# A two-block transformer forward pass: another order inside the attention steps, a second buffer for the copied transposes, late filling, and split bank waits

## The chip, the cores and the metric

The kernel runs on one core of a Trainium2 chip. The metric is the device time of one execution in microseconds (us). One launch computes the whole function. The five engines of the core have their own instruction queues and run in program order: TensorE (PE, with PEld for its weight loads), VectorE (DVE), ScalarE (ACT), GpSimd (POOL), and SyncE (SP), whose queue issues most of the transfers. They meet only through semaphores that count up.

## The reference, cut to what matters

Two transformer blocks of different kinds follow each other on a sequence of 512 tokens of width 1024, in float32. The parts that the change touches are the two attentions and what stands after them:

```
# block 1, 8 heads of 64 in 2 key/value groups; all 8 selection blocks are taken (min(16, 8)) and the
# window of 512 covers the whole sequence, so two of the three branches are plain causal attentions
s = einsum('bqgrd,bgqkld->bgrqkl', qc, ksel) * scale ; p = masked_softmax(s, m_sel)      # selected
s = einsum('bqgrd,bkgd->bgrqk', qc, kwc) * scale     ; p = masked_softmax(s, m_win)      # window
return gc[..., 0:1] * o_cmp + gc[..., 1:2] * o_sel + gc[..., 2:3] * o_win
x = x + (gate_pool * y_pool + gate_nsa * y_nsa) @ w_out
gate_pre, val = split(rms_norm(x) @ w_up) ; x = x + (silu(conv3(gate_pre)) * val) @ w_down

# block 2: a gated delta rule in 4 heads, and 8 heads of causal banded attention with a bias by distance
qkv = silu(conv4(concat(qa, ka, va)))
s = einsum('bqhd,bkhd->bhqk', qc, kc) * scale + bias ; p = softmax(s) ; o = einsum(..., p, vc)
mix = sigmoid(ga) * (oa @ w_branch_a) + sigmoid(gb) * (ob @ w_branch_b) ; x = x + mix @ w_out
u = conv3(rmsnorm(x) @ w_up) + b ; x = x + (silu(gate) * up) @ w_down ; return rmsnorm(x)
```

## The kernel before, in words

Activations lie transposed: features on the 128 partitions, the 512 tokens along the row. A weight matrix comes in chunks, each a column of 128x128 tiles for one output tile of 128 features. To keep float32 accuracy each product is made of three matmuls over a high and a low half (`product`, lines 1569 to 1580): high weights by high activations (L1576), high weights by low activations (L1577), low weights by high activations (L1578). A chunk of eight contraction tiles is 24 matmuls of 512 columns. For each chunk SP loads `w_raw` (`load`, L562), ACT makes `w_hi` (`high`, L739), and DVE or POOL makes `w_lo` (`low`, L540); each of these tiles has two slots, so a chunk's load, high and low wait for the chunk two before it. The order of all this is written out by hand, with one function per stage and engine.

The PSUM banks are ACC (0 and 1, chunk results), BS (2, 3), BT (4, 5) and BO (6, 7).

`attention` is written once per engine (PE L1669, ACT L835, DVE L1176) and used twice: att1 has 24 units (4 pairs of heads, 3 sets of query blocks, 2 branches), att2 has 12. A unit passes through a pipeline of steps; in step s

- PE makes the scores of unit s into BS (L1678), then the value products of unit s-3 from `at_pt` into BO (L1697, and L1690 for the compressed branch), then the transposes of unit s-2 from `at_p` into BT (L1667), and then some pieces of filling;
- DVE adds the mask and takes the row maxima of unit s (L1186), scales them (L1190, semaphore `shifted`), and weighs the exponentials of unit s-1 (L1196, L1204 or L1207, `weighted`);
- ACT makes the exponentials of unit s into `at_p`, which has two slots (L844, waits for `shifted` of s and, for the slot, for the transposes of unit s-2), and then copies the transposes of unit s-2 from BT to `at_pt`, which has one buffer (L853, waits for the value products of unit s-3; semaphore `fetched`).

The filling is chunks of other linear layers (gates of the merges, and in block 2 the projections of its own attention), laid between the steps of latency-bound stages. PE does it in pieces of a quarter chunk, six matmuls (`late` and `fill`, L1582); `fill_plan` (L43) spreads the pieces over the steps: att1 has 30 pieces on 24 steps, att2 19 on 12. In the last three steps, where PE has only transposes and values left, there is none. DVE copies a finished chunk to a stage tile and SP stores it to DRAM.

After the attentions comes `merge`: eight chunks of 24 matmuls, each of two halves into BS and BS+1, whose results DVE multiplies by sigmoid gates that SP has fetched back from DRAM into `sg` (two slots). On SP (L600 to L625) the order is: load chunk 0; store a filled chunk; wait for the stores; fetch the gates of 0 and of 1; load chunk 1; store the last two filled chunks; and from then on gates and load in turn. ACT does, after its attention, `high` of merge chunk 1, then the first sigmoid (L799), then `high` of chunk 2. The low half of merge chunk 1 is POOL's. PE may write BS for chunk 1 when DVE has read it for chunk 0 (`y_pool_done`).

At the end of `ffn` (L1664) PE waits until DVE has read both ACC banks of the last unit, and before `in2z` (L1842) until DVE has read the last `in2c` bank; the stage that follows begins with bank ACC, and takes bank ACC+1 one unit later.

## Time and profile before

| | us |
|---|---|
| median of 3 runs | 1627.44 (1626.38 to 1628.12) |
| the profiled execution | 1629.67 |
| its span in the trace | 1627.9 |
| PE busy in the span | 1550.2 (95%) |
| DVE, ACT, POOL busy | 919.4 (56%), 570.8 (35%), 180.8 (11%) |
| chain that ended last | PE 80%, DVE 10%, ACT 4%, issue 3% |

PE's busy time is the union of overlapping matmuls, each of which shows a start and a modelled end; the starts of 512-column matmuls follow each other every 0.23 us in a full stretch. An idle figure in brackets at a timeline row is the time for which the engine stood still before it, with the work that released it. Att1 lies from 192.5 to 317.5 us, att2 from 1096 to 1159.3 us.

### The profile page before, as it was taken

The page shows a single profiled execution, that of the slowest core. Times are in us where ns is not written, and L with a number is a line of the kernel's source. Part 1 is how long each engine was busy: PE and PEld are TensorE (multiplying, and loading weights), DVE is VectorE, ACT ScalarE, POOL GpSimd, SP SyncE. Part 2 cuts the span into 40 slices and gives each one's busy share as a digit, 9 for nine tenths or more (in the row PEclk, how much of TensorE's full clock was granted, in tenths as well). Part 3 has the DMA queues.
Part 4 walks back from the last instruction along what each step waited for, and adds up shares of the span by engine and source line. Part 5 has one row for each costly group of instructions (what it writes and reads, how often), then busy time and mean ns, then how long its engine had stood idle before and what let it go on. Part 6 is the DMA issues. An engine that isn't in the chain of part 4 may idle for free.

```text
span 1627.9 us, 21109 instructions
## 1 busy us (share of the span) xinstructions
PE 1550.2 (95%) x7702; PEld 1233.0 (76%) x7702; DVE 919.4 (56%) x1430; ACT 570.8 (35%) x872; POOL 180.8 (11%) x92
## 2 busy tenths in 40 slices
PE   5998899899999999999999989989999999999997
PEld 4876666688888888888777668766788877877885
DVE  5139565465666666333763562337566787787323
ACT  5134355543433333222324413235544223223221
POOL 2437111100000000000001243132100000000000
PEclk9999899999999999999999999999999999999998
DMA  6322111252322223222222241162242222223221
GB/s 223 142 104 97 58 59 40 72 181 91 104 90 91 103 103 105 93 102 75 91 101 89 93 128 66 46 220 104 84 151 96 97 90 90 103 90 110 92 104 70
DMA packets 57090, 164.77 MB, mean 101 GB/s; under 512 B 11696, under 2 KB 11960, under 8 KB 56896
## 3 DMA queue, kind: packets, MB, share of 16 engines
q1 hardware_dynamic: 51616, 157.67, 27.6%
q10 hardware_dynamic: 5408, 6.21, 1.2%
q8 instruction: 43, 0.70, 0.2%
q14 instruction: 23, 0.19, 0.0%
HBM read 148.89 MB, written 14.96 MB: 101 GB/s over the span
## 4 chain that ended last, share of the span: by engine, by line
PE 80%; DVE 10%; ACT 4%; issue 3%; POOL 1%; DMA 0%; ACTq 0%; DVEq 0%
PE banks L1576 24%; PE banks L1578 23%; PE banks L1577 23%; PE banks L1667 2%; PE banks L1697 2%; ACT at_p L844 1%; PE banks L1678 1%; ACT at_pt L853 1%; DVE at_sm L1186 1%; DVE w_lo L543 1%; POOL w_lo L543 1%; DVE cols L1190 1%; DVE t_raw L1086 1%; DVE pool_pad L511 1%; PE banks L1958 0%
## 5 line engine op out<-in xcount | busy, mean ns | idle before, releaser
L1576 PE MATMUL banks<-h_hi,w_hi 128*128 128x512 f32 x1312 | 533.4, 407 | 31.9 <-POOL w_lo L543 20.7
L1578 PE MATMUL banks<-h_hi,w_lo 128*128 128x512 f32 x1312 | 514.3, 392 | 0.0
L1577 PE MATMUL banks<-h_lo,w_hi 128*128 128x512 f32 x1312 | 513.6, 391 | 0.0
L743 ACT ACTIVATE w_hi<-w_raw 128x1024 fp32r<-128x1024 f32 (+1 forms) x228 | 251.5, 1103 | 474.4 <-PE banks L1578 414.8
L1576 PEld LDWEIGHTS banks<-h_hi,w_hi 128*128 128x128 f32 x1312 | 248.1, 189 | 105.6 <-issue 26.7
L1578 PEld LDWEIGHTS banks<-h_hi,w_lo 128*128 128x128 f32 x1312 | 247.7, 189 | 53.6
L1577 PEld LDWEIGHTS banks<-h_lo,w_hi 128*128 128x128 f32 x1312 | 248.2, 189 | 52.6 <-issue 5.1
L543 DVE TENSOR_TENSOR w_lo<-w_raw,w_hi 128x1024 fp32r<-128x1024 f32 (+1 forms) x167 | 216.6, 1297 | 78.9 <-ACT w_hi L743 78.9
L543 POOL TENSOR_TENSOR w_lo<-w_raw,w_hi 128x1024 fp32r<-128x1024 f32 x61 | 148.4, 2433 | 434.2 <-ACT w_hi L743 434.1
L1576 PE MATMUL banks<-act_hi,w_hi 128*128 128x512 f32 x352 | 137.2, 390 | 1.6 <-DVE t_raw L1086 0.8
L1578 PE MATMUL banks<-act_hi,w_lo 128*128 128x512 f32 x352 | 137.0, 389 | 0.0
L1577 PE MATMUL banks<-act_lo,w_hi 128*128 128x512 f32 x352 | 136.9, 389 | 0.0
L844 ACT ACTIVATE at_p<-at_sm,cols 128x128 f32<-128x128 f32 (+2 forms) x96 | 53.0, 553 | 77.4 <-DVE cols L1190 51.4
L1109 DVE TENSOR_TENSOR X<-X,banks 128x512 f32<-128x512 f32 (+1 forms) x32 | 22.0, 688 | 99.9 <-PE banks L1578 99.9
L1576 PEld LDWEIGHTS banks<-act_hi,w_hi 128*128 128x128 f32 x352 | 66.1, 188 | 15.8 <-DVE t_raw L1086 1.2
L1578 PEld LDWEIGHTS banks<-act_hi,w_lo 128*128 128x128 f32 x352 | 66.1, 188 | 13.8
L1577 PEld LDWEIGHTS banks<-act_lo,w_hi 128*128 128x128 f32 x352 | 66.1, 188 | 13.8
L811 ACT ACTIVATE act_hi<-t_gate 128x512 f32 (+1 forms) x44 | 27.8, 632 | 133.0 <-DVE t_gate L1172 133.0
L808 ACT ACTIVATE t_gate<-t_gate 128x512 f32<-128x512 f32 x44 | 27.9, 633 | 112.3 <-DVE t_gate L1154 112.3
L1086 DVE TENSOR_TENSOR t_raw<-banks,rms_inv 128x512 f32<-128x512 f32 x66 | 45.4, 689 | 33.4 <-PE banks L1578 26.2
L700 POOL MEMSET x_inv<- 128x2048 f32 x1 | 1.8, 1815 | 523.5 <-DVE p2a L1086 523.5
L1069 DVE TENSOR_TENSOR act_lo<-t_gate,act_hi 128x512 f32 (+1 forms) x44 | 30.5, 692 | 39.8 <-ACT act_hi L811 39.8
(285 smaller groups left out, 1777.3 us busy)
## 6 DMA issues: line engine op xcount, KB each, us to landing
w_raw<-in_w_up SPq DMA_DIRECT2D x88, 512.0 KB, 3.5
w_raw<-in_w_fill SPq DMA_DIRECT2D x44, 512.0 KB, 3.5
w_raw<-in_w_down SPq DMA_DIRECT2D x32, 704.0 KB, 3.9
late_scratch<-stage SPq DMA_DIRECT2D x44, 256.0 KB, 2.1
w_raw<-in_w_mix SPq DMA_DIRECT2D x16, 512.0 KB, 4.3
sg<-late_scratch SPq DMA_DIRECT2D x16, 512.0 KB, 3.8
w_raw<-in_w_out SPq DMA_DIRECT2D x16, 512.0 KB, 3.5
w_raw<-in_w_in SPq DMA_DIRECT2D x15, 512.0 KB, 3.5
```

Source lines behind the costliest of these rows:

```text
L543: eng.tensor_tensor(w_lo[:, c.slot, 0:kt * P], w_raw[:, c.slot, 0:kt * P], w_hi[:, c.slot, 0:kt * P], ALU.subtract).then_inc(lo_ready, 1)
L743: act.activation(w_hi[:, c.slot, 0:kt * P], w_raw[:, c.slot, 0:kt * P], ACT.Copy)\
L808: act.activation(t_gate[:, j, :], t_gate[:, j, :], ACT.Silu).then_inc(silu_done[b], 1)
L811: act.activation(act_hi[:, lin(j, 2, i), :], t_gate[:, j, :], ACT.Copy).then_inc(act_hh[b], 1)
L844: act.activation(a.p[:, s % 2, half, off:off + w], a.sm[:, half, off:off + w], ACT.Exp, bias=a.nbias[:, c:c + 1], scale=DH ** -0.5, accum_ ...
L1069: return dve.tensor_tensor(out_, a, b, ALU.subtract)
L1086: return dve.tensor_tensor(dst, src, rms_inv[:, :], ALU.mult)
L1576: pe.matmul(dst, w_h, hi[:, kr, :], start=first and n == 0, stop=False)
L1577: pe.matmul(dst, w_h, lo[:, kr, :], start=False, stop=False)
L1578: mm = pe.matmul(dst, w_l, hi[:, kr, :], start=False, stop=last and n == len(ks) - 1)
L1667: return pe.transpose(dst, src, ident[0:n, 0:n])
L1697: mm = pe.matmul(banks[rows(half), BO + j % 2, i * P:(i + 1) * P], v_tile(j, b, half, k), a.pt[:, half, off + k * P:off + (k + 1) * P], st ...
```

## The change

In PE's attention the order of a step becomes scores (s), filling, transposes (s-2), value products (s-3). `at_pt` gets two buffers by the unit's parity, so ACT's copy of unit u waits for the value products of unit u-2 in place of u-1. The filling goes on through the three last steps on PE, ACT and DVE: the same 30 and 19 pieces, on 27 and 15 steps. In block 2 the second buffer of `at_pt` shares its place with the second slot of the gates tile `sg2`, so SP waits for all value products of att2 (`summed`) before it fetches the gates of merge tile 1; what SP issues after that, the load of merge chunk 1 first, stands behind this wait. The waits for both banks at three stage borders (up1 to down1, in2c to in2z, up2 to down2) become one wait per bank, ahead of the first product that writes it.

```diff
-                            ("unit", 12, 19, 12)])
+                            ("unit", 15, 19, 15)])
...
-                            ("unit", 24, 30, 24)])
+                            ("unit", 27, 30, 27)])
...
-        at1_pt = area("at1_pt", [P, 2, T], F32, 74)
+        at1_pt = [area("at1_pt", [P, 2, T], F32, 74), area("at1_pt_odd", [P, 2, T], F32, 96)]
...
-        at2_pt = area("at2_pt", [P, 2, T], F32, 96)
+        at2_pt = [area("at2_pt", [P, 2, T], F32, 96), area("at2_pt_odd", [P, 2, T], F32, 20)]
...
                                 sp.wait_ge(late_stored[b][half], 16 * (first_gate + j_ + 1))
+                            if b == 1 and j_ == 1:
+                                sp.wait_ge(att2.summed, len(att2.pairs))
                             gates(j_, j_)
...
-                        wait(act, a.summed, u)
+                        wait(act, a.summed, u - 1)
...
-                    if serve and s < n:
+                    if serve and s < n + 3:
                         serve("unit", s)
...
-            def linear(name, n, used, per=1, mean=True):
+            def linear(name, n, used, per=1, mean=True, banks_free=None):
...
+                    if banks_free and isinstance(i, int) and i == 0:
+                        pe.wait_ge(banks_free[0], banks_free[1 + j])
...
-                pe.wait_ge(conv_done[b], steps * (FK - 1) + 5)
+
+            def ffn_banks(b, steps):
+                return conv_done[b], steps * (FK - 1) + 1, steps * (FK - 1) + 5
...
+                    fill("unit", s)
+                    u = s - 2
+                    if 0 <= u < n:
+                        for half in range(2):
+                            pe.wait_ge(a.weighted, a.half_done(u, half))
+                            wait(pe, a.fetched, 2 * (u - 1) + half + 1 if u else 0)
+                            ... transposes of unit u
                     u = s - 3
                     if 0 <= u < n:
                         ... value products of unit u, now from a.pt[u % 2]
-                    u = s - 2
-                    if 0 <= u < n:
-                        ... the transposes stood here
-                    if fill and s < n:
-                        fill("unit", s)
...
-            residual("down1", 2, act_hi, act_lo, act_hl[0])
+            residual("down1", 2, act_hi, act_lo, act_hl[0], ffn_banks(0, 5))
...
-            pe.wait_ge(cv_done, 5 * 11 + 1)
-            linear("in2z", 2, copied["in2z"], mean=False)
+            linear("in2z", 2, copied["in2z"], mean=False, banks_free=(cv_done, 5 * 10 + 1, 5 * 11 + 1))
...
-            residual("down2", 4, act_hi, act_lo, act_hl[1])
+            residual("down2", 4, act_hi, act_lo, act_hl[1], ffn_banks(1, 8))
```

## Rows read from the trace of the kernel before

**Rows 1.** Waits, 190 to 325 us: who for whom, total us, times, longest
```profile
PE banks L1697 <- ACT at_pt L853: 9.2, 10, 2.1
PE banks L1667 <- DVE at_p L1204: 2.1, 1, 2.1
ACT at_p L844 <- PE banks L1667: 22.6, 11, 3.0
```

**Rows 2.** Waits, 1095 to 1180 us
```profile
PE banks L1697 <- ACT at_pt L853: 2.6, 4, 0.9
PE banks L1667 <- DVE at_p L1207: 0.8, 1, 0.8
```

**Rows 3.** Windows: stretch, length, busy by engine (count), PEclk, DMA share, GB/s
```profile
192.50:317.50 125.00, 113.01 (x804) 77.32 (x804) 77.74 (x251) 66.59 (x189) 19.06 (x8) 0.99 0.16 56
1096.00:1159.30 63.30, 59.42 (x418) 41.69 (x418) 39.71 (x128) 35.28 (x98) 11.88 (x5) 1.00 0.20 72
262.00:264.00 2.00, 2.00 (x16) 1.67 (x13) 0.20 (x1) 0.15 (x1) 0.00 (x0) 0.50 0.03 8
319.00:321.00 2.00, 2.00 (x5) 1.61 (x6) 0.39 (x1) 1.97 (x3) 1.91 (x1) 0.50 0.34 131
```

**Rows 4.** Timeline of PE in att1: start, length, line, operation, idle before
```profile
217.83 0.93 PE L1678 MATMUL banks<-p 64*128 64x128 f32 x8
220.46 0.48 PE L1576 MATMUL banks<-h_hi,w_hi 128*128 128x512 f32 x1
222.03 0.93 PE L1678 MATMUL banks<-p 64*128 64x128 f32 x8
225.11 1.09 PE L1697 MATMUL banks<-at_pt,v_nat 128*64 128x128 f32 x16 [2.15 <-ACT at_pt L853]
...
260.94 1.97 PE L1697 MATMUL banks<-at_pt,v_nat 128*64 128x128 f32 x16 [1.93 <-ACT at_pt L853]
```

**Rows 5.** Timelines of POOL, DVE and ACT over the same step
```profile
219.78 2.40 POOL L543 TENSOR_TENSOR w_lo<-w_raw,w_hi 128x1024 fp32r<-128x1024 f32 x1 [11.94 <-ACT w_hi L743]
...
220.03 2.18 DVE L1190 TENSOR_SCALAR cols<-cols 128x4 f32<-128x4 f32 x1
...
224.00 1.05 ACT L853 ACTIVATE at_pt<-banks 128x512 f32<-128x512 f32 x2
```

**Rows 6.** Timeline of PE, end of att2 and start of mix2
```profile
1158.11 1.09 PE L1697 MATMUL banks<-at_pt,v_nat 128*64 128x128 f32 x16 [0.80 <-ACT at_pt L853]
1160.63 0.50 PE L1576 MATMUL banks<-oa_hi,w_hi 128*128 128x512 f32 x1 [1.42 <-DVE ob_lo L1069]
```

**Rows 7.** Timeline of SP's queue around mix2
```profile
1136.16 0.34 SPq L564 DMA_DIRECT2D w_raw<-in_w_mix  x1
...
1167.27 0.41 SPq L605 DMA_DIRECT2D sg<-late_scratch  x1
```

**Rows 8.** Timelines of ACT, POOL and DVE in mix2
```profile
1159.75 1.05 ACT L743 ACTIVATE w_hi<-w_raw 128x1024 fp32r<-128x1024 f32 x1
1162.11 1.06 ACT L799 ACTIVATE sg<-sg 128x1024 f32<-128x1024 f32 x1
1172.41 1.06 ACT L743 ACTIVATE w_hi<-w_raw 128x1024 fp32r<-128x1024 f32 x1 [2.90 <-DMA w_raw<-in_w_mix]
...
1160.87 2.40 POOL L543 TENSOR_TENSOR w_lo<-w_raw,w_hi 128x1024 fp32r<-128x1024 f32 x1 [10.22 <-ACT w_hi L743]
...
1163.78 0.69 DVE L1127 TENSOR_TENSOR mt<-banks,sg 128x512 f32<-128x512 f32 x1 [2.60 <-PE banks L1578]
1168.08 1.22 DVE L543 TENSOR_TENSOR w_lo<-w_raw,w_hi 128x1024 fp32r<-128x1024 f32 x1 [0.19 <-ACT w_hi L743]
```

**Rows 9.** Timeline of PE at the borders of up1 and up2
```profile
647.81 0.39 PE L1578 MATMUL banks<-h_hi,w_lo 128*128 128x512 f32 x1
648.98 0.50 PE L1576 MATMUL banks<-act_hi,w_hi 128*128 128x512 f32 x1 [0.78 <-DVE t_val L1086]
...
1495.45 0.50 PE L1576 MATMUL banks<-act_hi,w_hi 128*128 128x512 f32 x1 [0.78 <-DVE t_raw L1086]
```

More of the change, by code:

```diff
@@ L849, in attention @@
                         w = a.width(u)
-                        wait(act, a.summed, u)
+                        wait(act, a.summed, u - 1)
                         for half in range(2):
                             act.wait_ge(a.flipped, 2 * u + half + 1)
-                            act.activation(a.pt[:, half, 0:w], banks[:, BT + half, 0:w], ACT.Copy)\
+                            act.activation(a.pt[u % 2][:, half, 0:w], banks[:, BT + half, 0:w], ACT.Copy)\
                                 .then_inc(a.fetched, 1)
-                    if serve and s < n:
+                    if serve and s < n + 3:
                         serve("unit", s)
@@ L1213, in attention @@
                         sub(a.o_lo[:, j, :], bank(BO + j % 2), a.o_hi[:, j, :]).then_inc(a.low, 1)
-                    if s < n:
+                    if s < n + 3:
                         serve("unit", s)
@@ L1624, in linear, with residual @@
                         norm(n)
-            def residual(name, n, hi, lo, split_):
+            def residual(name, n, hi, lo, split_, banks_free=None):
                 nchunk, kt = INFO[name][1], INFO[name][2]
@@ L1629, in residual @@
                     wait(pe, x_done, lin(DK * (n - 1) + j - 1, 2, i) if not (isinstance(i, int) and i == 0) else 0)
+                    if banks_free and isinstance(i, int) and i == 0:
+                        pe.wait_ge(banks_free[0], banks_free[1 + j])
                     for q in range(nchunk):
@@ L1663, in ffn, with attention @@
                             norm(n)
-                pe.wait_ge(conv_done[b], steps * (FK - 1) + 5)
+            def ffn_banks(b, steps):
+                return conv_done[b], steps * (FK - 1) + 1, steps * (FK - 1) + 5
             def turn(dst, src, n=P, last=None):
                 return pe.transpose(dst, src, ident[0:n, 0:n])
-            def attention(a, q_tile, k_tile, v_tile, first_values=None, fill=None):
+            def attention(a, q_tile, k_tile, v_tile, first_values, fill):
                 n = len(a.pairs)
@@ L1681, in attention @@
                                     mm.then_inc(a.scored, 1)
+                    fill("unit", s)
[4 more added lines that the diff above has]
+                            wait(pe, a.fetched, 2 * (u - 1) + half + 1 if u else 0)
+                            for k in range(a.width(u) // P):
+                                mm = turn(banks[:, BT + half, k * P:(k + 1) * P],
+                                          a.p[:, u % 2, half, k * P:(k + 1) * P])
+                            mm.then_inc(a.flipped, 1)
                     u = s - 3
@@ L1697, in attention @@
                                     mm = pe.matmul(banks[rows(half), BO + j % 2, i * P:(i + 1) * P],
-                                                   v_tile(j, b, half, k), a.pt[:, half, off + k * P:off + (k + 1) * P],
+                                                   v_tile(j, b, half, k), a.pt[u % 2][:, half, off + k * P:off + (k + 1) * P],
                                                    start=opens and k == 0, stop=end and k == i)
                         mm.then_inc(a.summed, 1)
-                    u = s - 2
-                    if 0 <= u < n:
-                        for half in range(2):
-                            pe.wait_ge(a.weighted, a.half_done(u, half))
-                            wait(pe, a.fetched, 2 * (u - 1) + half + 1 if u else 0)
-                            for k in range(a.width(u) // P):
-                                mm = turn(banks[:, BT + half, k * P:(k + 1) * P],
-                                          a.p[:, u % 2, half, k * P:(k + 1) * P])
-                            mm.then_inc(a.flipped, 1)
-                    if fill and s < n:
-                        fill("unit", s)
             linear("in1", 0, copied["in1"])
@@ L1986, in _ @@
             attention(att2, lambda j: p2b[:, j, :], lambda j, b: p2b[:, 4 + j, :],
-                      lambda j, b, half, k: v2_nat[:, k, j * P + half * DH:j * P + (half + 1) * DH], fill=fill)
+                      lambda j, b, half, k: v2_nat[:, k, j * P + half * DH:j * P + (half + 1) * DH], None, fill)
             pe.wait_ge(att2.low, 4)
```

## The prediction, written before the changed kernel was run

> **What bounds the kernel now.** I read the busy table first: PE is busy for 95% of the span, no other engine is above 56%, and the chain of waits runs 80% over PE. So a microsecond in which PE stands still is a microsecond of the result, and work on another engine counts only when PE waits for it. The waits sorted by who waited for whom, cut to the two attentions, say where it stands still. In att1 PE waits 9.2 us in ten places for ACT's copy of the transposes before the value products, and once 2.1 us for the first weighed exponentials [rows 1]; in att2 2.6 and 0.8 us [rows 2]. The windows show PE busy for 113.0 of 125 us and 59.4 of 63.3 us, with DVE and ACT at 53 to 63% [rows 3]: neither is the bound of a stage, it is the length of the path from scores to copied transposes that sometimes exceeds the work that PE has meanwhile.
>
> The timeline shows the mechanism in one step. Scores of unit 6 end at 218.76; DVE's scaling of the maxima takes 2.18 us because POOL's `w_lo` began 0.25 us before it; ACT therefore starts its exponentials late and ends the copy of unit 4 at 225.05 [rows 5]. That is 6.3 us after the scores. PE comes to the value products of unit 4 one step later, 4.20 us after the scores (217.83 to 222.03), and stands still for 2.15 us [rows 4]. This step has one filling piece, 1.57 us (220.46 to 222.03).
>
> **The change, part by part.**
>
> *Order and second buffer.* Before, between the scores of s and the use of the copy of unit s-2 lies one step. Now the value products come last, after the filling and transposes of the next step. What needs the copy first is then the transposes of unit s-1 in step s+1, since BT is still one buffer: their first half waits for the first half of the copy. The distance is one step plus one filling piece, 4.20 + 1.57 = 5.8 us; the first half of the copy was ready at 224.00 + 0.53, also 5.8 us after the scores [rows 4, 5]. So the worst wait of att1 comes to about nothing, and those of ten that were shorter vanish. The second buffer alone moves nothing: ACT's copy never waited for `summed`, it is what makes the later value products harmless. The 2.1 us at the first transposes lies behind a filling piece too, so about 0.7 stays (2.1 - 1.4).
>
> Against this stands the price of putting the filling ahead of the transposes: ACT's exponentials of s wait for the transposes of s-2 (slot of `at_p`), which is already 22.6 us of ACT's idle time in 11 places [rows 1]. Before, these transposes ended about 1.7 us after the scores, now one piece and the first half of the transposes is 2.0 us, in a step with two pieces 3.5 us. Then 1.8 us of exponentials and half a copy of 0.5 end at 4.3 to 5.8 us, and the next step's transposes come after 5.8, or 7.2 where this step has two pieces. I leave 1.2 us of small waits in att1 for steps where both meet, and 0.3 in att2. Bounds: nothing left (0) and half of all waits left (5.6 and 1.7).
>
> Att1: 9.2 + 2.1 - 0.7 - 1.2 = 9.4 us. Att2: 2.6 + 0.8 - 0.3 = 3.1 us.
>
> *Clock.* After the wait of 1.93 us the granted clock was 0.50, the 1.2 GHz level (window 262 to 264) [rows 3]; 16 value products took 1.97 us there against 1.09 at 225.11 [rows 4]. It lasted from those products at 260.94 to the window's end, 3 us, so half of that, 1.5 us, was lost and should come back with the wait. A second such episode (319 to 321) [rows 3] lies at the start of the merge behind the wait for the last attention output, which stays. I count the first, and keep the second, of about the same price, as a chance.
>
> *Filling in the last steps.* The number of pieces is unchanged, so PE's work is. What it does is included above: the two last waits of 0.8 us of each attention (one of them stands in [rows 6]) are among those counted. Steps with two pieces fall from 6 to 3 in att1 and rise nowhere. The last chunk is finished just ahead of the last values, and ACT's `high` for merge chunk 1 stands behind its last output copy in either kernel, so nothing moves there. Merge chunk 0 has its high and low made some 4 us before the end.
>
> *SP's wait.* This is the part that costs. Take T = 1159.20 as the end of the value products [rows 6]. Before, the load of merge chunk 1 was issued at 1136.16 [rows 7], 23 us before T. Now it stands behind the wait for T and behind the gates of tile 1. A pair of gates and load of the same sizes took from the issue at 1167.27 to ACT's start on it at 1172.41, 5.14 us [rows 7, 8]. So ACT begins `high` of chunk 1 at T + 5.2 in place of T + 0.55 (1159.75). Behind it on ACT stands the first sigmoid, which with its table ended 2.37 us after that `high` (1160.80 to 1163.17, [rows 8]): now T + 8.6. Then DVE's product of 0.69 must free bank BS: T + 9.4. POOL's `w_lo` of 2.40 us ends at T + 8.7, a little earlier. PE is ready for chunk 1 at T + 1.43 + 24 x 0.228 = T + 6.9. It waits 2.5 us. Also behind SP's wait are two stores of filled chunks and the load of chunk 2; the last store waited for DVE after T before as well, and the load of chunk 2 moves by under 1 us, to where its slot becomes free. If the clock drops in that pause, 1.5 us more; if the transfers are as quick as a lone one, 3.4 us by SP's next load, 1.3 less at most. I take 2.5, bounds 0.8 and 4.0. The first of the two gates is issued before the wait and is not late.
>
> *Bank waits.* At three borders PE stood still for 0.78 us (648.98, 1495.45 and a like one at 838.41). From start to start it was 1.17 us where the stream has 0.23 [rows 9], so each is worth 0.78 to 0.94 and a slower first matmul. DVE had made the next chunk's low half before, and bank ACC had been read some 5 us earlier, so nothing takes the place. 3 x 0.95 = 2.9 us. Bank ACC+1 is wanted only after a whole unit, 5.5 us and more, while DVE reads it within 0.8. Bounds 2.3 and 3.1.
>
> *POOL against DVE.* In the trace each of POOL's `w_lo` calls, eight in att1 and five in att2 [rows 3], can hold one DVE instruction back by up to 2.2 us [rows 5].
>
> The Trainium skill, "SBUF — State Buffer", section "Who interferes with whom", says that the port pair shared by DVE and GpSimd is an exclusive lock, and that the one that comes second stands still for the other's whole instruction. By that rule, the trace agrees (0.17 us became 2.18 beside a POOL instruction of 2.40), the change removes no collision, and if each of the thirteen fell on the scaling of the maxima and left 0.3 us, 3.9 us would stay in place of my 1.5, and the time would be 2.4 us above my forecast.
>
> **Sum.** 9.4 + 3.1 + 1.5 - 2.5 + 2.9 = 14.4 us. Against the profiled execution, 1629.67 (span 1627.9 and 1.8 around it), this gives 1615.3. The median of the runs is 2.2 us below that execution, so the forecast for the median is 1627.44 - 14.4 = 1613.0.
>
> **The rivals.**
>
> 1. *The exponentials become the wait.* Filling ahead of the transposes delays ACT in every step, and with collisions the copy is late for the transposes of the next step. For it: 22.6 us of ACT's idle time already ends with these transposes [rows 1]. Against it: the next transposes are themselves a piece later. Price: half of the waits left, 5.6 + 1.7 in place of 1.9 + 0.3, so 5.1 less gain and, with some low clock, about 1619.
> 2. *All waits go and the clock stays up in both places.* No residual (2.2 with the first transposes' 0.7 covered as well) and 1.5 for the merge's start: 1609.
> 3. *Slower: SP's wait starts a late train in mix2.* Each later load stands behind gates that wait for DVE's read of an earlier chunk, so the late first load could make each of the eight chunks late by 2.5 us, 20 us, with the clock falling in some of the pauses, four times 1.5. Together 26 us, against the 17 us gained elsewhere: 9 us slower, 1636. The point from which it decides is the slack at the end of a chunk's preparation: `w_lo` of chunk 2 ended at 1169.30 [rows 8] and PE wanted it at 1160.63 + 2 x 5.46 = 1171.55, 2.25 us later. As chunks 2 and 3 also get PE's own delay of 2.5 us as slack, the train should die at once.
> 4. *The gain does not come:* the wait moves wholly to the transposes, as the path from scores to copy is what limits a step. PE busy at 90% of att1 [rows 3] leaves only the bank waits and a lost 2.5: 1627.
>
> **Chances.** Forecast 64% (own range 1610 to 1616), rival 1 18%, rival 2 10%, rival 3 4%, rival 4 4%. A measurement of this kernel tells about 0.2%, 3.3 us, from no change. Faster by over that: 92%; within it 4%; slower 4%. The range is 1607 to 1622, which holds the bounds of the unknown costs with rivals 1 and 2.
>
> **What would show it.** Right: no wait of L1697 for `at_pt` over 0.3 us; small waits of L1667 for `at_pt`; att1 about 114 us long in place of 125 and att2 about 60; filling matmuls in the last three steps; in mix2 one wait of PE of 2 to 3 us, the load of chunk 1 issued right after the last value product, and none at chunks 2 and 3; no pause at the three borders. Wrong: waits of L1667 for ACT or DVE adding to over 5 us, a wait of over 1 us in mix2 after chunk 1, or mix2 without any wait.

## The result, and the profile of the changed kernel

The changed kernel takes 1617.18 us (median of 4 runs, 1613.74 to 1617.27), the kernel before beside it 1627.78 (4 runs, 1626.38 to 1628.14). The ratio is 0.9932, 95% interval 0.9919 to 0.9945: faster by 0.7%. The forecast was 1613.0, its range 1607 to 1622, so the result lies inside the range but outside the narrower 1610 to 1616. The profiled execution took 1617.22 us, its span is 1615.4, 12.5 less than before.

I cut the span by the starts of PE's work into stages, for every kernel of this study. The columns are: first attention; merge of tile 0; from there to the border before down1; down1 to the first state product of the delta rule; from there to the second attention; the second attention; the merge of tile 1; the rest, to the last product of down2. Behind that the span has 13.3 us more (13.5 in one kernel, 14.2 in two), which stand in no column.

```
                 att1   mix1  out1-up1  down1..state  ..att2  att2   mix2   rest
before          126.3   45.2    284.9      370.3       76.9   64.4   40.3   413.7
after           114.7   43.6    284.0      369.1       77.0   64.0   45.6   412.2
load first      114.7   43.7    284.0      368.7       77.0   64.0   40.8   412.3
free place      114.7   43.6    284.0      369.5       78.4   64.0   40.3   412.2
banks only      126.4   45.2    284.0      367.2       77.0   64.4   40.3   412.7
one buffer      115.6   43.6    284.0      366.2       76.9   64.0   45.3   412.7
no tail fill    115.3   43.7    283.9      369.5       77.0   62.4   44.0   412.1
fill between    119.7   43.6    284.0      365.6       77.0   67.0   45.6   412.2
old order att2  114.7   43.6    284.0      367.0       77.0   65.8   40.1   412.3
early high      114.6   43.6    284.0      367.1       76.9   62.8   40.2   412.3
pieces early    114.6   43.6    284.0      367.7       77.0   62.3   40.2   412.2
att2 no tail    114.5   43.6    284.0      367.6       76.9   64.3   40.3   412.1
tail fill only  121.5   43.7    284.9      368.5       78.4   67.5   40.1   413.8
two buf no tail 114.6   43.6    284.0      367.5       77.0   62.3   40.3   412.2
```

Work ahead of att1 (187.4 to 192.6 us) and the stage with down1 differ by up to 5 us between kernels whose code is the same there. The stage ahead of att2 is 1.4 us longer in experiments 2 and 11: there the granted clock fell to the 1.2 GHz level behind a pause of 2.3 us that others passed at full speed. The remaining stages repeat to about 0.1. So each experiment is judged by its stage first, from one profiled execution of each kernel. From before to after: att1 -11.6, mix1 -1.6, att2 -0.4, mix2 +5.3, out1 to up1 -0.9, rest -1.5, one border of 0.9 inside the scattering stage; together -11.6. The other 0.9 of the span's 12.5 lies in the scatter.

First the busy table of the page (busy us, share of the span, instructions):

```profile
PE 1551.5 (96%) x7702; PEld 1237.5 (77%) x7702; DVE 917.0 (57%) x1430; ACT 570.7 (35%) x872; POOL 180.6 (11%) x92
```

Waits of 190 to 325 us, PE's, then the ACT line that answers to [rows 1] (who for whom, total us, times, longest):

```profile
PE banks L1578 <- POOL w_lo L543: 1.7, 1, 1.7
PE banks L1578 <- issue: 1.5, 1, 1.5
PE banks L1686 <- ACT pc_t L950: 0.7, 1, 0.7
...
ACT at_p L846 <- PE banks L1675: 27.6, 17, 3.2
```

The 9.2 us for `at_pt` and the 2.1 for `at_p` of [rows 1] are both gone. ACT now stands behind the later transposes for 27.6 us in 17 places in place of 22.6 in 11, as the price of the order was put, and PE never waits for what comes of it. One wait is new: the filling of step 2 now stands ahead of the transposes and comes before POOL has made its low half. The 1.5 us put down to "issue" is the pause ahead of the first merge product, as before the change.

The windows (length, busy us and count of PE, PEld, DVE, ACT, POOL, granted clock, DMA share, GB/s) of att1, att2, and of mix2 behind its wait:

```profile
191.90:305.10 113.20, 111.52 (x804) 78.05 (x804) 77.92 (x251) 66.50 (x187) 18.93 (x8) 1.00 0.18 61
1080.30:1143.00 62.70, 61.35 (x418) 43.40 (x418) 36.83 (x128) 35.07 (x97) 11.93 (x5) 1.00 0.15 51
1153.00:1156.00 3.00, 2.44 (x7) 2.02 (x8) 2.29 (x4) 1.68 (x3) 0.00 (x0) 0.69 0.37 118
1156.00:1158.00 2.00, 2.00 (x7) 1.54 (x7) 1.23 (x2) 0.84 (x1) 0.00 (x0) 0.61 1.03 394
```

Against [rows 3], PE idles 1.7 us of att1 in place of 12.0, with the same 804 matmuls, and is busy 1.5 us less: the time at the 1.2 GHz level is back. In att2 the idle time falls from 3.9 to 1.35 us, but the same 418 matmuls are busy for 61.35 us in place of 59.42. Waits have moved inside groups of matmuls. The waits of 1075 to 1170 us:

```profile
PE banks L1578 <- DVE mt L1129: 3.5, 1, 3.5
PE banks L1578 <- DVE ob_lo L1071: 1.4, 1, 1.4
PE banks L1686 <- DVE cols L1188: 0.7, 1, 0.7
PE banks L1686 <- ACT v_nat L1056: 0.7, 1, 0.7
PE banks L1675 <- DVE at_p L1209: 0.4, 1, 0.4
```

The timelines of PE, DVE and POOL in att2 (start, length, operation, idle before) show where they went:

```profile
1085.19 1.37 PE L1686 MATMUL banks<-p2b 64*128 64x512 f32 x4
1088.48 1.01 PE L1675 MATMUL banks<-consts,at_p 128*128 128x128 f32 x6 [0.35 <-DVE at_p L1209]
1089.55 1.53 PE L1686 MATMUL banks<-p2b 64*128 64x128 f32 x8
1126.42 1.60 PE L1686 MATMUL banks<-p2b 64*128 64x512 f32 x4 [0.74 <-DVE cols L1188]
...
1085.70 3.19 DVE L1209 TENSOR_SCALAR at_p<-at_p,cols 128x128 f32<-128x128 f32 x4
1124.60 0.69 DVE L1071 TENSOR_TENSOR ob_lo<-banks,ob_hi 128x512 fp32r<-128x512 f32 x1 [3.67 <-ACT ob_hi L863]
1125.81 0.55 DVE L1188 CUSTOM_DVE_ANT_0 at_sm<-banks,rel 128x384 f32<-128x384 f32 x1
1127.16 1.01 DVE L1209 TENSOR_SCALAR at_p<-at_p,cols 128x128 f32<-128x128 f32 x4
...
1085.70 2.38 POOL L543 TENSOR_TENSOR w_lo<-w_raw,w_hi 128x1024 fp32r<-128x1024 f32 x1 [7.99 <-ACT w_hi L745]
```

The score group at 1089.55 has the form that took 0.93 us in [rows 4] and takes 1.53; scores have one pair of banks (BS), and DVE's masks read it late. Twice DVE is late: behind the weighing at 1085.70, 3.19 us beside POOL in place of the 1.01 at 1127.16, and at 1124.60, where it waits 3.67 us for ACT's `ob_hi` while the masks of step 10 stand behind that on its queue. (The scores at 1085.19 took 1.37 us in place of the 1.13 of this form elsewhere; that began before POOL's instruction did, behind masks that had waited for ACT's exponentials.) Both attentions' waits for the copy are gone.

In mix2, SP's queue, ACT, DVE and PE:

```profile
1143.03 0.38 SPq L605 DMA_DIRECT2D sg<-late_scratch  x1
1143.46 0.46 SPq L564 DMA_DIRECT2D w_raw<-in_w_mix  x1
1143.97 1.29 SPq L568 DMA_DIRECT2D late_scratch<-stage  x2
...
1149.20 1.06 ACT L745 ACTIVATE w_hi<-w_raw 128x1024 fp32r<-128x1024 f32 x1 [5.63 <-DMA w_raw<-in_w_mix]
1150.28 1.28 ACT L801 ACT_TABLE_LOAD   x1
1151.57 1.06 ACT L801 ACTIVATE sg<-sg 128x1024 f32<-128x1024 f32 x1
...
1152.72 0.69 DVE L1129 TENSOR_TENSOR mt<-banks,sg 128x512 f32<-128x512 f32 x1 [7.82 <-POOL w_lo L543]
...
1153.56 0.47 PE L1578 MATMUL banks<-oa_hi,w_hi 128*128 128x512 f32 x1 [3.47 <-DVE mt L1129]
```

The chain is the predicted one, link by link, but longer: ACT's `w_hi` starts 6.17 us after the gates' issue, where the pair in [rows 7, 8] took 5.14, and PE goes on 10.6 us after the last values, not 9.4. Behind the wait the clock is low (the two windows above). The border waits of [rows 9] have no counterpart in the trace of after.

### The profile page after: what moved, and what is told of

Its sections match the earlier page's. It is cut to its first block, busy times and chain, and to the rows that moved or that the text cites. A ratio compares the mean times of both kernels' runs of the same rounds, so it can differ in the third digit from the quotient of the medians.

```text
span 1615.4 us, 21110 instructions
## 1 busy us (share of the span) xinstructions
PE 1551.5 (96%) x7702; PEld 1237.5 (77%) x7702; DVE 917.0 (57%) x1430; ACT 570.7 (35%) x872; POOL 180.6 (11%) x92
## 4 chain that ended last, share of the span: by engine, by line
PE 82%; DVE 9%; issue 4%; ACT 3%; POOL 1%; DVEq 0%; DMA 0%; ACTq 0%; POOLq 0%
PE banks L1578 24%; PE banks L1580 23%; PE banks L1579 23%; PE banks L1675 2%; PE banks L1686 2%; PE banks L1715 2%; POOL w_lo L543 1%; DVE w_lo L543 1%; DVE t_raw L1088 1%; DVE pool_pad L511 1%; ACT w_hi L745 1%; PE banks L1928 0%; PE banks L1964 0%; PE banks L1943 0%; PE banks L1955 0%
## 5 line engine op out<-in xcount | busy, mean ns | idle before, releaser
L1578 PEld LDWEIGHTS banks<-act_hi,w_hi 128*128 128x128 f32 x352 | 66.1, 188 | 13.5
L846 ACT ACTIVATE at_p<-at_sm,cols 128x128 f32<-128x128 f32 (+2 forms) x96 | 52.9, 552 | 62.2 <-PE banks L1675 38.4
```

Of the source, the lines that this page charges most:

```text
L846: act.activation(a.p[:, s % 2, half, off:off + w], a.sm[:, half, off:off + w], ACT.Exp, bias=a.nbias[:, c:c + 1], scale=DH ** -0.5, accum_ ...
L1578: pe.matmul(dst, w_h, hi[:, kr, :], start=first and n == 0, stop=False)
```

## The experiments

Kernels are the changed one with the edit shown, except where "before" is named. "At" stands for the median. The ratio is to the kernel before, measured beside it: its median was 1629.04 us for 1 to 4, 1628.62 for 5 to 8, 1627.74 for 9 to 11 and 1623.82 for 12. The changed kernel itself was not measured again there, so totals of different groups are compared by their ratios, and less safely than the stages.

**1. The load of merge chunk 1 ahead of SP's wait.**

```diff
                             if b == 1 and j_ == 1:
+                                load(chunk(name, 0, 1), name, DK)
                                 sp.wait_ge(att2.summed, len(att2.pairs))
...
-                    load(chunk(name, i, j), name, DK)
+                    if not (b == 1 and isinstance(m, int) and m == 1):
+                        load(chunk(name, i, j), name, DK)
```

> The changed kernel, but SP loads merge chunk 1 of block 2 ahead of its wait for the last value product; only the gates of tile 1 stay behind that wait. Theory: the 3.5 us pause of PE in mix2 and the 1.7 us of low clock behind it come from the late load (it lands 6.2 us after the last values, and behind it stand high, table, sigmoid and DVE's product). Then mix2 has no pause and the time falls by about 5.3 us against the changed kernel, to 1612. Rival: the late gates or the stores that now start together with them are what holds mix2; then a pause of 2 us or more stays and the time is 1615 to 1617.

At 1609.66 us (1607.91 to 1611.0), ratio 0.9888 (0.9872 to 0.9904). Mix2 is 40.8 us in place of 45.6. The timelines of SP and ACT in this kernel:

```profile
1138.16 0.38 SPq L605 DMA_DIRECT2D sg<-late_scratch  x1
1138.59 1.86 SPq L568 DMA_DIRECT2D late_scratch<-stage  x2
...
1138.66 1.05 ACT L747 ACTIVATE w_hi<-w_raw 128x1024 fp32r<-128x1024 f32 x1
1139.73 1.28 ACT L803 ACT_TABLE_LOAD   x1
1141.02 1.06 ACT L803 ACTIVATE sg<-sg 128x1024 f32<-128x1024 f32 x1
```

The gates are still issued after the last values, and ACT's `w_hi` and sigmoid come at once: the second gates' lateness costs at most 0.5 us. What SP's wait costs is the late load, 4.8 of 5.3 us; the rival, a pause of 2 us or more, did not come.

**2. The odd buffer in two free pieces, no wait on SP** (`cols2` makes room for it; the lines that index the pieces are left out).

```diff
-area("at2_pt_odd", [P, 2, T], F32, 20)
+(area("at2_pt_odd0", [P, T], F32, 56), area("at2_pt_odd1", [P, T], F32, 86))
...
-                            if b == 1 and j_ == 1:
-                                sp.wait_ge(att2.summed, len(att2.pairs))
```

> The changed kernel, but the second at_pt buffer of att2 lies in two free pieces of the arena, so SP does not wait for the value products at all. Theory: the same 1612 as with the load ahead of the wait, since the gates of tile 1 are wanted only 10 us later. Rival: the gates' own delay costs too; then this one is 1 to 2 us faster than the one with only the load ahead.

At 1611.24 us (1610.36 to 1612.34), ratio 0.9895 (0.988 to 0.991). Mix2 40.3, as before the change. So all 5.3 us come from the wait, and from nothing in the new order; against experiment 1 the gates' own delay is worth 0.5.

**3. Before, with the split bank waits alone** (the same edit of `linear` and `residual` as in the change).

```diff
+                    if banks_free and isinstance(i, int) and i == 0:
+                        pe.wait_ge(banks_free[0], banks_free[1 + j])
...
-                pe.wait_ge(conv_done[b], steps * (FK - 1) + 5)
...
-            pe.wait_ge(cv_done, 5 * 11 + 1)
```

> The kernel before with nothing but the split bank waits at the three borders. Theory: three pauses of 0.78 us go with their restart, 2.7 to 2.9 us less than before: about 1624.6. Rival: the next wait (a low half, or bank ACC+1) takes their place: within 0.5 us of before, 1627.4.

At 1625.46 us (12 runs, 1623.93 to 1628.68), ratio 0.9983 (0.9972 to 0.9993): 2.8 us, interval 1.1 to 4.6. Out1 to up1 -0.9 and the rest -1.0, the attentions and merges untouched. The third border lies in the scattering stage; its wait of 0.78 us is gone too. The term of 2.9 agrees with this.

**4. One buffer of copied transposes.**

```diff
-                        wait(act, a.summed, u - 1)
+                        wait(act, a.summed, u)
...
-                            act.activation(a.pt[u % 2][:, half, 0:w], banks[:, BT + half, 0:w], ACT.Copy)\
+                            act.activation(a.pt[0][:, half, 0:w], banks[:, BT + half, 0:w], ACT.Copy)\
```

> The changed kernel with one at_pt buffer in both attentions: ACT's copy of unit u waits for the value products of u-1 again; order of the step, filling, SP's wait stay. Theory: the gain of the attentions comes from the place of the value products behind the filling; the copy ends about 4 us after the scores in either case, and then the transposes have a score and a filling piece, 2.5 us, before they want BT. At most 1.5 us slower than the changed kernel: 1617 to 1618.7. Rival: the second buffer carries the gain; then the copy becomes the wait of every step, and the time is 1623 or more.

At 1614.91 us (1612.27 to 1617.0), ratio 0.9917 (0.9902 to 0.9932). Att1 115.6 in place of 114.7, att2 64.0 as it was. The second buffer is worth 0.9 us in att1; in att2, where its place costs 5.3, it is worth nothing in this order with the filling to the end.

**5. No filling in the last three steps.**

```diff
-                            ("unit", 15, 19, 15)])
+                            ("unit", 12, 19, 12)])
...
-                            ("unit", 27, 30, 27)])
+                            ("unit", 24, 30, 24)])
...
-                    fill("unit", s)
+                    if s < n:
+                        fill("unit", s)
```

> The changed kernel with the filling as before: 30 and 19 pieces on 24 and 12 steps, none in the last three. Order, two buffers, SP's wait and bank waits stay as changed. Theory: the two waits of 0.8 us at the end of each attention come back and nothing else, so att1 takes 116.3 us in place of 114.7 and att2 65.5 in place of 64.0; with the early low clock of mix1 back, 1.5 us more: 1620 to 1622. Rival: the filling in the tail gave nothing, since waits in the middle take its place: 1617.

At 1613.88 us (1610.44 to 1615.36), ratio 0.991 (0.9893 to 0.9927). Att1 is 0.6 longer, att2 1.6 shorter: for att2 theory and rival both fell. With the same pieces in 12 steps and not 15, the first twelve of att2 are covered better than they are in the changed kernel, and the last three lose less than that: all score groups are at their full speed and the wait of 0.74 us is gone, while 0.46 us for a low half and 0.94 for the copy in the last steps are new. Mix2, which still has SP's wait, takes 44.0. Its pause is the same, but the clock did not fall behind it:

```profile
1151.85 0.47 PE L1578 MATMUL banks<-oa_hi,w_hi 128*128 128x512 f32 x1 [3.41 <-DVE mt L1129]
...
1152.00:1155.00 3.00, 3.00 (x14) 2.45 (x15) 2.24 (x4) 2.34 (x3) 0.00 (x0) 1.00 0.51 152
```

**6. Scores, transposes, filling, values.**

```diff
-                    fill("unit", s)
                     u = s - 2
...
+                    fill("unit", s)
                     u = s - 3
```

> The changed kernel with the steps in the order scores, transposes, filling, values. The exponentials' slot is then free earlier, but from the scores to the next transposes lies only one step. Theory of the prediction: what ends the waits is that the transposes, which want bank BT, come one filling piece later; here they come 4.1 us after the scores and the copy of the transposes is ready after 4.3 to 5.8, so waits of transposes for at_pt of 0.2 to 1.7 us appear, about 6 us in att1 (120 us long) and 2 to 3 in att2 (66): 1623 to 1626. Rival: it is the place of the value products alone; then att1 stays at 115 us and the time at 1617.

At 1623.24 us (1616.59 to 1625.3), ratio 0.9968 (0.9954 to 0.9982). The waits of PE in its att1, and one place of its att2:

```profile
PE banks L1675 <- ACT at_pt L855: 3.2, 5, 1.2
PE banks L1675 <- DVE at_p L1206: 2.1, 1, 2.1
PE banks L1675 <- ACT at_pt_odd L855: 1.9, 1, 1.9
...
1090.41 1.54 PE L1675 MATMUL banks<-consts,at_p 128*128 128x128 f32 x6 [1.89 <-DVE at_p L1209]
```

Att1 119.7, att2 67.0, as the theory said. With the filling behind the transposes the wait moves to them, since they have one pair of banks (BT). That the filling stands ahead of them is worth 5.0 us in att1. Of the 3.0 us in att2 about 1.7 is clock: behind the pause of 1.89 us the granted clock was 0.54 from 1090 to 1092, and six transposes took 1.54 us in place of 1.01. So the place of the filling is worth about 1.3 there.

**7. Att2 in the old order with one buffer, filling kept to its last step, no SP wait.** This tells what thinner filling does by itself. Att1 keeps the new order; for att2 the three blocks stand as values, transposes, filling.

```diff
-        at2_pt = [area("at2_pt", [P, 2, T], F32, 96), area("at2_pt_odd", [P, 2, T], F32, 20)]
+        at2_pt = [area("at2_pt", [P, 2, T], F32, 96)]
...
-                        wait(act, a.summed, u - 1)
+                        wait(act, a.summed, u - len(a.pt) + 1)
```

> The changed kernel with the order and the single buffer of before in att2 alone (the filling still reaches its last step), so SP has no wait. Theory: the new order brings nothing in att2, as its steps wait for the masks now: att2 takes 63 to 64.5 us in either order, and mix2 is 40.3 us in place of 45.6, so about 1611. Rival: the new order is worth the forecast 3 us in att2 too; then att2 takes 66 to 67 us and the time is 1614.

At 1610.05 us (1606.95 to 1611.07), ratio 0.9886 (0.9868 to 0.9905). Att2 65.8. PE's waits there, beside 2.6 and 0.8 us in [rows 2], and two rows of its timeline:

```profile
PE banks L1734 <- ACT at_pt L853: 3.7, 6, 1.4
PE banks L1673 <- DVE at_p L1207: 1.9, 1, 1.9
...
1127.11 1.09 PE L1734 MATMUL banks<-at_pt,v_nat 128*64 128x128 f32 x16 [1.38 <-ACT at_pt L853]
...
1141.82 0.39 PE L1576 MATMUL banks<-oa_hi,w_hi 128*128 128x512 f32 x1
```

So spreading the same 19 pieces over 15 steps costs 1.4 us in the old order (64.4 to 65.8), and the new order then wins 1.8 (65.8 to 64.0). My expectation that the order brings nothing in att2 fell; the two nearly cancel. The last row shows something that I had overlooked: in the old order the filling stands last in a step, so the last piece also fills the pause ahead of the merge (1.42 us in [rows 6]), and mix2 begins here without one. The new order gives this cover up: its last step ends with value products, and the pauses of 1.5 and 1.4 us ahead of the two merges stay. A last step with the filling behind the values was not run.

**8. One buffer in att2, no SP wait, ACT's last-output `high` at the start of the step.**

```diff
                 for s in range(n + 5):
+                    u = s - 4
+                    if 0 <= u < n and u % a.per_tile == a.per_tile - 1:
+                        j = u // a.per_tile
+                        act.wait_ge(a.summed, u + 1)
+                        act.activation(a.o_hi[:, j, :], bank(BO + j % 2), ACT.Copy).then_inc(a.high, 1)
                     if s < n:
                         act.wait_ge(a.shifted, s + 1)
```

> New order in both attentions, two buffers in att1 and one in att2, no wait on SP, and ACT makes the high half of a finished output tile at the start of its step in place of the end. Theory: the wait of DVE for that high half (3.7 us before the masks of unit 10 of att2) is what makes the scores of unit 11 wait (0.74 us, and 0.5 inside the group); with it early, att2 takes 62 to 63 us, att1 stays at 114.7, mix2 at 40.3: 1609 to 1610. Rival: the masks are late for other reasons (POOL beside DVE, the early steps); then att2 stays at 64 us and the time at 1611.5.

At 1607.28 us (1604.84 to 1608.48), ratio 0.987 (0.9853 to 0.9888). Att2 62.8. DVE at the place where it had waited 3.67 us:

```profile
1117.46 0.68 DVE L1069 TENSOR_TENSOR ob_lo<-banks,ob_hi 128x512 fp32r<-128x512 f32 x1
...
1119.05 0.56 DVE L1186 CUSTOM_DVE_ANT_0 at_sm<-banks,rel 128x384 f32<-128x384 f32 x1 [0.31 <-PE banks L1684]
```

`ob_lo` follows without a wait, and the masks wait for the scores alone. That is the 1.2 us, since neither the one buffer (4) nor the missing wait (2) changes att2.

**9. Version 8, with att2's pieces 1, 2, 2, then ten of 1, then 2, 2.**

```diff
-            behind = start + num * (i + 1) // den
+            behind = start + (sum(num[:i + 1]) if den is None else num * (i + 1) // den)
...
-                            ("unit", 15, 19, 15)])
+                            ("unit", 15, (1, 2, 2) + 10 * (1,) + (2, 2), None)])
```

> The kernel with the early high half (new order, one buffer in att2, no wait on SP), with att2's 19 pieces laid 1, 2, 2, then ten times 1, then 2, 2 over its 15 steps. Theory: thinner filling opened waits in att2's first steps, where values and transposes do not cover yet (scores of units 2 and 3 held 0.24 and 0.6 us, transposes 0.35); with two pieces each in steps 1 and 2 these go while the tail stays covered: att2 takes 61.5 to 62.2 us in place of 62.8. Rival: it is the total of work in the later steps that counts; then att2 takes 62.8 or more.

At 1605.65 us (1603.8 to 1609.04), ratio 0.9862 (0.9848 to 0.9877). Att2 62.3, 0.5 less than version 8, and just outside the 61.5 to 62.2 expected: the three waits of the first steps are gone, but PE waits 0.47 us for the low half of a filling piece and 0.52 for a copy in their place. The totals of versions 8 and 9 can't be told apart.

**10. Version 8, with att2's filling on its first 12 steps.** The edit is that of 5, for att2 alone.

```diff
-                    if s < n + 3:
+                    if s < n + (3 if a is att1 else 0):
                         serve("unit", s)
```

> The kernel with the early high half, with att2's filling on its first twelve steps as before and att1's on all 27. Theory: in att2 the filling of the last three steps is taken from steps that need it and gives nothing net: with the early high half att2 takes 61.5 to 62.5 us, no longer than with the filling in the tail (62.8), and the time is 1606 to 1607. Rival: with the late high half gone the middle needs no thick filling, the tail's two waits come back, and att2 takes 64 us, the time 1608.5.

At 1612.85 us (1610.3 to 1614.87), ratio 0.9912 (0.99 to 0.9925). Att2 64.3: 1.5 longer than version 8, where the same edit of the changed kernel made it 1.6 shorter. The theory fell, and the rival had att2 right. PE in the last steps:

```profile
1133.85 0.90 PE L1673 MATMUL banks<-consts,at_p 128*128 128x128 f32 x6 [0.95 <-ACT at_pt L858]
...
1136.24 1.07 PE L1673 MATMUL banks<-consts,at_p 128*128 128x128 f32 x8 [0.68 <-ACT at_pt L858]
...
1139.29 1.09 PE L1714 MATMUL banks<-at_pt,v_nat 128*64 128x128 f32 x16 [1.18 <-ACT at_pt L858]
```

With one buffer the copy waits for the values before it, and with no filling PE has nothing to do meanwhile. Experiment 5 had two buffers.

**11. Before, with nothing changed but the filling, which goes on to the last step** (its plan on 27 and 15 steps and the work of ACT and DVE for it go with it, as in the change).

```diff
-                    if fill and s < n:
+                    if fill:
                         fill("unit", s)
```

> The kernel before with nothing changed but the filling, 30 and 19 pieces on 27 and 15 steps. Theory: in the old order each step's filling is what covers the way to the copy, so thinner filling lengthens the waits in the middle by more than the tail's 1.6 us: att2 takes 65.8 us in place of 64.4, and att1 128 to 130 in place of 126.3: 1629 to 1632. Rival: the tail's waits go and nothing takes their place: att1 124.7, att2 62.9, and 1624.

At 1621.92 us (1618.84 to 1623.69), ratio 0.9962 (0.995 to 0.9974): the expectation missed by its sign. Att1 is 121.5, 4.8 us shorter, mix1 1.5 shorter, att2 67.5, 3.1 longer. PE's waits in att1, and the end of att2:

```profile
PE banks L1697 <- ACT at_pt L853: 5.6, 11, 1.4
...
1138.28 1.68 PE L1697 MATMUL banks<-at_pt,v_nat 128*64 128x128 f32 x16 [1.39 <-ACT at_pt L853]
```

In the old order the spread filling takes 3.6 of the 9.2 us in att1, and 1.5 more is the pause ahead of the first merge product, which the last pieces fill. In att2 it adds the waits of 7, and 16 products took 1.68 us in place of 1.09, the clock low behind a pause of 1.39. In experiment 7 the same products behind a pause of 1.38 took 1.09; this episode is the 1.7 us by which att2 is longer here than there.

**12. Version 10 with two buffers in att2, the odd one in free pieces as in 2.**

```diff
-        at2_pt = [area("at2_pt", [P, 2, T], F32, 96)]
+        at2_pt = [area("at2_pt", [P, 2, T], F32, 96),
+                  (area("at2_pt_odd0", [P, T], F32, 56), area("at2_pt_odd1", [P, T], F32, 86))]
```

> The version whose att2 fills in its first 12 steps only, now with two buffers of copied transposes in att2 as well, the odd one in two free pieces of the scratch area, so without SP's wait. Theory: without filling work in the last three steps the copy has to wait there for the value products that read the buffer before, and PE in turn for the copy; with one buffer that was 0.68 us before the transposes and 1.18 us before the last values. With two buffers both waits go: att2 62.4 us in place of 64.3 us, only the wait of 0.95 us of the transposes for the first half of the copy stays. Mix2 stays at 40.3, att1 at 114.5. Rival: the second buffer is worth nothing in att2, as in the changed kernel itself, where its removal left att2 at 64.0: then att2 stays at 64.3. Time: near the two best so far, 1605 to 1610 us, by the theory; 1608 to 1613 by the rival.

At 1607.16 us (1604.55 to 1608.0), ratio 0.9885 (0.9864 to 0.9906). Att2 62.3 as the theory said. The two waits are gone; of the last steps the 0.94 us stays, and there is one of 0.47 us early on:

```profile
1085.08 0.50 PE L1580 MATMUL banks<-h_hi,w_hi 128*128 128x512 f32 x1 [0.47 <-POOL w_lo L547]
...
1133.59 0.90 PE L1677 MATMUL banks<-consts,at_p 128*128 128x128 f32 x6 [0.94 <-ACT at_pt_odd L862]
...
1135.22 1.09 PE L1677 MATMUL banks<-consts,at_p 128*128 128x128 f32 x8
...
1137.11 1.09 PE L1718 MATMUL banks<-at_pt_odd,v_nat 128*64 128x128 f32 x16
```

The second buffer and the filling at the end do one and the same job. Either alone is enough in att2: 62.8 with filling and one buffer, 62.3 with two buffers and none, 64.3 with neither. Experiment 5, which has two buffers and no filling at the end but the late `high`, took 62.4, so beside thick filling the early `high` is worth next to nothing.

## Why the prediction was right, and where it was not

*The order and att1: right.* Predicted 9.4 us and 1.5 of clock, measured 11.6. No wait was left where I left 1.2 us, while one of 1.68 came at the first filling piece; this piece stands ahead of the transposes whose exponentials I had put at 0.7, so it took their place. Experiment 6 shows that 5.0 of the 11.6 us hang on the filling standing ahead of the transposes; 6.6, the 1.5 of clock among them, stay when it stands behind them. The second buffer has 0.9 of it (4). For the filling at the end I had counted the two last waits of 0.8 us and nothing more; in the old order it is worth 4.8 us (11), once the new order stands 0.6 (5). The parts don't add.

*The clock.* The episode behind [rows 4]'s wait of 1.93 us went as forecast. The one at the start of mix1, kept as a chance, went as well: mix1 lost 1.6 us in every kernel that shortened att1, the old order of 11 among them. Why its clock stays up is not shown: except in 11 the pause ahead of it, 1.47 us, is still there, and the clock fell behind it in two kernels (before and 3) and in none of eleven others.

*Att2: the step that failed.* Predicted 3.1 us, measured 0.4. "The number of pieces is unchanged, so PE's work is" is true, but I costed their distribution at nothing. Nineteen pieces in 15 steps leave fewer steps with two, and each of these steps was cover: 1.4 to 1.6 us (7 against before, 5 against after; in 7 net of the 1.4 us pause ahead of mix2 that it fills). A second part I had not named at all: DVE works in order, and its `ob_lo` for the output of ACT stands ahead of the next masks, 1.2 us (8). The two don't add either: the filling alone brings att2 to 62.4 (5), the early `high` alone to 62.8 (8), and both to 62.3 (12), 2.1 under before. The rest up to 3.1 can be read in 12: 0.94 us for the copy in the last steps and 0.47 for a low half that POOL has not made when the filling, now earlier in its step, wants it; I had left 0.3 in all.

The Trainium skill, "SBUF — State Buffer", section "Who interferes with whom", says that the port pair shared by DVE and GpSimd is an exclusive lock, and that the one that comes second stands still for the other's whole instruction. The trace agrees (3.19 us beside a POOL instruction of 2.38, 1.01 without one). But of the thirteen calls that I priced by it, one held PE by more than 0.2 us in the attentions, at 1088.48 and 1089.55: 0.35 and 0.60, about 1.0 us in all where that rule gave 3.9.

*SP's wait: right in its chain, wrong in its size.* Predicted 2.5 with bounds 0.8 and 4.0, measured 5.3. About 1.0 is the transfers: I took the pair of [rows 7, 8] as it was, but here the two stores that had also stood behind the wait start 0.5 us after the load, 1.5 MB in all, and the load lands later. That the stores are the cause is argued from these rows, not tested. And 1.7 is the clock, which I had named and left out of the sum: from 1153.56 the first 12 products took 4.40 us to the next start, in place of 2.74 (12 x 0.228). It did not come in 5, where mix2 took 44.0.

*Bank waits: right*, 2.9 against 2.8 in experiment 3.

*The rivals.* 1, the exponentials as the new wait: it did not come in att1; in att2 new waits did come, 0.7 and 0.4 us beside those inside groups, but through DVE's masks and weighing, and part of them behind ACT's `ob_hi`. 2, all waits and the clock: true of att1 and mix1. 3, a late train: the wait of chunk 1 is the only one of mix2, so the train died at once as worked out. 4, no gain: refuted.

In sum, terms against measurement: att1 and its clock 10.9 and 11.6; mix1 0 and 1.6; att2 3.1 and 0.4; mix2 -2.5 and -5.3; borders and rest 2.9 and 3.3. That is 14.4 forecast and 11.6 found. The total is nearer than its parts by luck: att2 and mix2 fell short by 2.7 and 2.8 us, and the others brought 2.7 more than forecast. By the medians it is 10.6; the difference of 1.0 is within the scatter of the stages that the change doesn't touch. Of the signs that I had set, no pause at the borders, no wait for the copy at the value products and none at chunks 2 and 3 of mix2 came true; att2 at about 60 us and a wait of 2 to 3 us in mix2 did not, and small waits of the transposes for `at_pt` didn't appear.

## What to carry to other kernels

Filling work is cover, and its amount for each step is part of the change: in the old order, spreading the same pieces over more steps took 1.4 us from one attention (7) and gave 4.8 to the other (11). It also covers the pause that follows it, so look at what a new order leaves bare: here the pauses of 1.5 and 1.4 us ahead of the merges. Before a buffer is put where it needs a wait on a load queue, ask what else could give the same slack: in att2 one buffer with filling to the end cost nothing, the wait 5.3 us. And where an engine works in order, look at what stands ahead of the instruction that frees the bound engine's bank; moving ACT's `high` to the start of its step was worth 1.2 us with the pieces on 15 steps. It was worth next to nothing with them on 12, so such gains have to be measured together.

Version 9, with one buffer in att2, no wait on SP, the early `high` and pieces early and late, has the lowest ratio: 1605.65 us, 1.4% under the kernel before. Versions 8 (0.987) and 12 (0.9885) can't be told from it.

## What the runs showed of the hardware

The granted clock falls after quite different pauses of PE: behind 3.47 us it was 0.69 and 0.61 over the next windows, behind 1.93 us 0.50 [rows 3], behind 1.39 us (11) products took 1.5 times their time, while behind 2.15 us [rows 4] and 1.68 us (after, in att1) they ran at full speed. The same pause in the same place went either way: 1.38 and 1.39 us before the same products (7 full, 11 low), 1.89 us before the same transposes (7 and 11 full, 6 low), 3.4 us in mix2 (5 full, 4 low). The length of a pause alone does not tell whether it is followed by the 1.2 GHz level.

I counted the pauses of over 1.2 us from 190 to 330 and from 1040 to 1200 us in all fourteen traces. Of the four of about 3.4 us three were followed by the low level; of the 79 shorter ones, 1.22 to 2.31 us, eleven were. An episode cost 1.4 to 1.7 us where PE was the bound. So a pause of 3.4 us on the path is better priced with that on top as the likely case, and a shorter one with it as a chance of about one in seven.
